# The experts' y in a convolutional decoder step: last two blocks kept on the chip, the rest added to x1 by accumulating DMAs

## What is computed

```python
x = x + concat(z_a, z_b) @ w_out                       # called x1 below
t = rmsnorm(x, g_ffn)                                  # called h2 below
grp  = argmax(coarse_logits)                           # 1 of 4 groups of 8 experts
top2 = top_k(fine_logits[grp], 2)
combine[token, expert] = softmax(top2) * p_grp         # two weights per token
out  = sum_e combine[:, e] * ((silu(t @ w_gate[e]) * (t @ w_up[e])) @ w_down[e])
y    = rmsnorm(x + out, g_final)
```

## Time and profile before

| | us |
|---|---|
| median of 3 runs | 563.7 (563.47 to 567.64) |
| the profiled execution's own time | 564.33 |
| its span in the profile | 562.6 |
| busy in the span: PE / DVE / POOL / ACT | 492.4 / 246.6 / 189.4 / 100.4 |
| mean granted TensorE clock, as a share of full speed | 0.966 |
| read from / written to DRAM | 134.47 MB / 13.17 MB |

### The profile page before, as it was taken

How to read it: one execution, slowest core, us unless ns; L and a number is a source line. 1 busy time by engine, 2 the same in 40 slices (tenths; PEclk the granted TensorE clock), 3 DMA queues, 4 the chain that set the end, 5 groups by cost and what they waited for, 6 DMA issues and landing times.

```text
span 562.6 us, 9132 instructions
## 1 busy us (share of the span) xinstructions
PE 492.4 (88%) x3423; PEld 294.4 (52%) x3424; DVE 246.6 (44%) x496; ACT 100.4 (18%) x204; POOL 189.4 (34%) x283
## 2 busy tenths in 40 slices
PE   6999999999999999996889889898877686498974
PEld 3887777777776455553344444444433343244431
DVE  4139999999955112347222212222121212022245
ACT  5131111011125332333111011110110101011113
POOL 2013818837678001112333333332323313033100
PEclk9999999999999999995899999999999989599998
DMA  8994016000002990149597999999999999998077
GB/s 331 307 395 88 0 24 276 2 0 1 1 1 97 401 379 37 40 130 394 181 348 266 369 379 408 383 401 385 395 373 384 400 389 399 400 404 332 29 260 252
DMA packets 35504, 141.17 MB, mean 251 GB/s; under 512 B 10322, under 2 KB 10338, under 8 KB 23193
## 3 DMA queue, kind: packets, MB, share of 16 engines
q1 hardware_dynamic: 29194, 127.91, 60.0%
q0 software_dynamic: 4960, 9.45, 5.2%
q10 hardware_dynamic: 1327, 3.49, 1.7%
HBM read 134.47 MB, written 13.17 MB: 262 GB/s over the span
## 4 chain that ended last, share of the span: by engine, by line
PE 67%; DMA 16%; issue 6%; SPq 4%; DVE 3%; ACT 2%; POOL 1%; DVEq 0%; POOLq 0%; ACTq 0%
PE bank L1226 25%; DMA region_w<-in_w_up 10%; PE bank L1309 9%; PE bank L1422 8%; PE bank L1442 7%; PE bank L1417 7%; DMA region_w<-in_w_in 3%; SPq L390 3%; DMA slot<-y_rows 2%; PE bank L1219 2%; PE bank L1408 2%; PE bank L1182 1%; PE bank L1432 1%; PE bank L1335 1%; PE bank L1370 1%
## 5 line engine op out<-in xcount | busy, mean ns | idle before, releaser
L1226 PE MATMUL bank<-region_h,region_w 128*128 128x256 f32 (+1 forms) x576 | 140.6, 406 | 0.0
L1226 PEld LDWEIGHTS bank<-region_h,region_w 128*128 128x128 f32 x576 | 109.2, 190 | 29.8
L1111 DVE TENSOR_TENSOR ua<-ua,bank 128x128 f32<-128x128 f32 x30 | 8.6, 287 | 184.0 <-ACT ua L621 184.0
L1422 PE MATMUL bank<-region_w,z 128*32 128x256 f32 x512 | 46.2, 419 | 16.6 <-DMA region_w<-in_w_up 14.2
L1309 PE MATMUL bank<-region_w,z 128*128 128x512 f32 x128 | 56.7, 596 | 0.2 <-ACT z L566 0.2
L1442 PE MATMUL bank<-region_w,ua 128*32 128x512 f32 x344 | 51.9, 598 | 0.0
L774 POOL COPY gcol<-gidx 64x1 uint32 (+1 forms) x30 | 5.4, 178 | 136.0 <-DVE sb_rows L1102 136.0
L909 DVE SCALAR_TENSOR_TENSOR z<-ub,par,z 128x512 f32<-128x512 f32 x60 | 47.5, 791 | 0.0
L909 DVE SCALAR_TENSOR_TENSOR region_x<-ub,par,region_x 128x512 f32<-128x512 f32 x56 | 46.5, 830 | 0.0
L705 POOL TENSOR_TENSOR ub<-region_x 128x512 f32<-128x512 f32 x4 | 25.3, 6332 | 58.7 <-ACT ub L520 32.0
L1309 PEld LDWEIGHTS bank<-region_w,z 128*128 128x128 f32 x128 | 23.8, 190 | 28.0 <-issue 26.3
(11 more groups left out here) (231 smaller groups left out, 657.3 us busy)
## 6 DMA issues: line engine op xcount, KB each, us to landing
region_w<-in_w_down SPq DMA_DIRECT2D x21, 1024.0 KB
region_w<-in_w_gate SPq DMA_DIRECT2D x16, 1024.0 KB
region_w<-in_w_up SPq DMA_DIRECT2D x16, 1024.0 KB
region_w<-in_w_in SPq DMA_DIRECT2D x4, 2048.0 KB, 19.1
slot<-in_w_gate SPq DMA_DIRECT2D x6, 1024.0 KB
slot<-in_w_up SPq DMA_DIRECT2D x6, 1024.0 KB
slot<-in_w_down SPq DMA_DIRECT2D x6, 1024.0 KB
region_x<-in_w_up SPq DMA_DIRECT2D x5, 1024.0 KB
```

The costliest lines, as they stand in the source:

```text
L1226: ins = mm(ps[2 * bank + j][:, 0:LEN[j]], sec[name][:, k, c * P:(c + 1) * P], hT[:, k, CUT[j]], start=(k == 0), stop=(k == KC - 1))
L1422: ins = mm(ps[1][r0:r0 + H, 0:2 * P].rearrange("p (w f) -> p w f", w=2), xT[:, k, half * H:(half + 1) * H], wgu[i][:, :, k, h, :], start=( ...
```

## The change

Each (token, choice)'s weight is applied when ACT copies y out of PSUM, not at the end. For that, `w12` is transposed on PE, copied by DVE to `wT`, stored by ACT to `w_dram` (four DMAs), and POOL gathers 128 weights of 4 bytes for each block (`weigh`, `weights`). `y_dram` is filled with zeros early (from a strip of slot 0 that POOL sets to zero, so expert 0's weights wait for it), x1 is also stored to `x1_dram`, and `yg`, `diag` and the work of PE, DVE and POOL on them are gone. The last two blocks are not scattered: their y stays in `yblk`. As soon as the other blocks' y has landed, POOL issues ten accumulating DMAs that add `y_dram` rows to x1 in SBUF (`add_rows`), and, for the 128 rows of the last two blocks, gathers of x1, y(k = 0) and y(k = 1) into `late`, the latter two accumulating (`fetch_late`). PE adds the on-chip y of the two blocks with 0/1 matrices `same[b]` (four matmuls), DVE adds that to `late`, and these rows are normed and scattered over the stored outputs, after all five tiles' stores have landed: tiles 0 to 4 hold these tokens without the last two blocks' y until then. DVE works out the tokens' numbers (`ilast`, 15 small operations) before its loop.

Cut to its core:

```diff
 # SP
+            sp.wait_ge(s_zero, 1)
+            sp.dma_start(y_dram.rearrange("(i p) d -> p i d", p=P),
+                         zero.unsqueeze(1).to_broadcast([P, 2 * NTOK // P, D])).then_inc(s_yz, 16)
+            sp.wait_ge(s_yz, 16)
             for part in range(2):
                 load_part(0, part, 0)
...
+            def store_x1(t):
+                sp.wait_ge(s_x1, 2 * t + 2)
+                sp.dma_start(x1_dram[t * P:t * P + TROWS[t], :], x1[0:TROWS[t], t, :]).then_inc(s_x1d, 16)
+            for t in range(NT - 1):
+                store_x1(t)
             sp.wait_ge(s_o, NT)
             load_expert(3, 3)
+            store_x1(NT - 1)
...
-            sp.wait_ge(s_ysc[1], pairs * 16)
-            sp.wait_ge(s_ysc[0], (pairs + odd) * 16)
-            for t, k in ((0, 0), (0, 1), (2, 0), (1, 0), (2, 1), (1, 1), (4, 0), (4, 1), (3, 0), (3, 1)):
-                sp.dma_start(yg[k][t][0:TROWS[t], :], y_dram[k * NTOK + t * P:k * NTOK + t * P + TROWS[t], :])\
-                  .then_inc(s_yg[k][t], 16)
 # ACT
+            act.wait_ge(s_wT, 1)
+            for k in range(2):
+                act.dma_start(w_dram[...], wT[...]).then_inc(s_wd, 16)     # twice for each k
...
+                act.wait_ge(s_wg[b], q * 16 + 16)
-                nc.scalar.activation(yblk[b], ps[3][:, :], ACT.Copy).then_inc(s_yc, 1)
+                nc.scalar.activation(yblk[b], ps[3][:, :], ACT.Copy, scale=wcol[:, b:b + 1]).then_inc(s_yc, 1)
...
+            for t in range(NT):
+                if t == BY_DVE:
+                    act.wait_ge(s_sqd, 1)
+                else:
+                    act.wait_ge(s_acc[t], 32)
+                    nc.scalar.activation(junk[0][0:n, :], x1[0:n, t, :], ACT.Square, accum_out=...)
+                root(t, n, s_rms3)
+            act.wait_ge(s_latex, 2)
+            nc.scalar.activation(junk[0], late, ACT.Square, accum_out=...)
+            root(NT, P, s_rms3)
 # POOL
+            pool.memset(wcol[:, :], 0.0).then_inc(s_const, 1)
+            pool.memset(zero, 0.0).then_inc(s_zero, 1)
...
+            def weigh(b, rows):
+                pool.indirect_dma_start(wcol[:, b:b + 1], None, w_dram[:, :],
+                                        bass.IndirectOffsetOnAxis(ap=rows, axis=0), ...).then_inc(s_wg[b], 16)
+            def weights(g, b, count):
+                pool.tensor_copy(vcol[:, b:b + 1], vidx[:, bass.ds(g, 1)]).then_inc(s_vc, 1)
+                pool.wait_ge(s_vc, count)
+                pool.tensor_tensor(carry[:, 3:4], carry[:, 1:2], carry[:, 1:2], ALU.add)
+                weigh(b, vcol[:, b:b + 1])
...
+            pool.wait_ge(s_wd, 64)
+            for b in range(2):
+                weigh(b, vidx[:, b:b + 1])
...
             with pool.Fori(0, pairs - 1) as h:
                 for b in range(2):
                     pool.wait_ge(s_mv, h * 2 + (b + 3))
                     gather(h * 2 + (b + 4), b)
                     scatter(h * 2 + b, b, h * 2 + (b + 2))
+                    weights(h * 2 + (b + 2), b, h * 2 + (b + 1))
-            for b in range(2):
-                scatter_last(b, b, pairs * 2 + b)
...
+            pool.wait_ge(s_ysc[1], lastp * 16)
+            pool.wait_ge(s_ysc[0], (lastp + odd) * 16)
+            def add_rows(t, k):
+                pool.dma_start(x1[0:n, t, :], y_dram[r:r + n, :], accum_op=ALU.add).then_inc(s_acc[t], 16)
+            fetch_late(x1_dram[:, :], 0, NTOK - 1)
+            for t in range(NT):
+                add_rows(t, 0)
+                if t == 2:
+                    pool.wait_ge(s_late, 16)
+                    fetch_late(y_dram[:, :], 0, 2 * NTOK - 1, compute_op=ALU.add)
+            for t in range(NT):
+                pool.wait_ge(s_acc[t], 16)
+                add_rows(t, 1)
+                if t == 0:
+                    pool.wait_ge(s_late, 32)
+                    fetch_late(y_dram[:, :], 1, 2 * NTOK - 1, compute_op=ALU.add)
+            pool.wait_ge(s_out, 16 * NT)
+            pool.wait_ge(s_nlate, 1)
+            for i, (dst, rows) in enumerate(((y_prompt[0], SEQ), (y_sample..., NS * SL))):
+                pool.indirect_dma_start(dst, ...ilast[:, 2 + i:3 + i]..., late, None, ...)
 # DVE
+            dve.wait_ge(s_wT_ps, 1)
+            nc.vector.tensor_copy(wT[:, :], ps[6][0:2 * NT, 0:P]).then_inc(s_wT, 1)
...
+            for t in range(NT):
+                normed(t, TROWS[t], x1[0:TROWS[t], t, :], s_norm[t])
+                if t == 1:
+                    dve.wait_ge(s_late, 48)
+                    for j in range(2):
+                        nc.vector.tensor_tensor(half, half, ps[4 + 3 * j][:, :], ALU.add).then_inc(s_latex, 1)
+            normed(NT, P, late, s_nlate)
 # PE
-            keep_busy(24)
+            keep_busy(6)
+            pe.wait_ge(s_w12, 1)
+            tr(ps[6][0:2 * NT, 0:P], w12, ident[:, :]).then_inc(s_wT_ps, 1)
+            keep_busy(17)
```

More of the change, by code:

```diff
@@ L115, in build_step @@
         hidT = ua_t[:, 2 * P:3 * P]
-        yg = [[(SLOT0 if k == 0 else RW)[:, t * D:(t + 1) * D] for t in range(NT)] for k in range(2)]
+        zero = SLOT0[:, 0:D]
+        late = RW[:, 0:D]
+        junk = [RW[:, D:2 * D], RW[:, 2 * D:3 * D]]
         ident = sb("ident", [P, P])
@@ L135, in build_step @@
         st_p = pst
-        diag = [[pst[:, (2 * i + k) * P:(2 * i + k + 1) * P] for k in range(2)] for i in range(len(BY_PE))]
+        dtok = pst[:, 0:P]
+        same = [pst[:, (1 + b) * P:(2 + b) * P] for b in range(2)]
+        wT = pst[0:2 * NT, 3 * P:4 * P]
         hist_t = sb("hist_b", [P, D])
@@ L468, in _ @@
                 sp.dma_start(dst, x1[0:TROWS[t], t, :]).then_inc(s_out, 16)
+            for i in range(2):
+                sp.wait_ge(s_olate[i], 16)
             sp.wait_ge(s_hout, 16 * 5)
@@ L662, in _ @@
+            act.wait_ge(s_latex, 2)
+            nc.scalar.activation(junk[0], late, ACT.Square, accum_out=small[:, 16 + NT:17 + NT]).then_inc(s_sq3, 1)
+            act.wait_ge(s_sq3, squared + 1)
+            root(NT, P, s_rms3)
         @block.gpsimd
@@ new lines, in _ @@
+            for t in range(NT):
[6 more added lines that the diff above has]
+            pool.wait_ge(s_nlate, 1)
+            for i, (dst, rows) in enumerate(((y_prompt[0], SEQ), (y_sample.rearrange("s l d -> (s l) d"), NS * SL))):
+                pool.indirect_dma_start(dst, bass.IndirectOffsetOnAxis(ap=ilast[:, 2 + i:3 + i], axis=0), late, None,
+                                        bounds_check=rows - 1, oob_is_err=False).then_inc(s_olate[i], 16)
@@ L1129, in _ @@
                 block_of(pairs, 0)
+            dve.wait_ge(s_trow, 1)
+            for b in range(2):
+                nc.vector.tensor_scalar(same[b], ps[6][:, 0:P], vlast[:, 3 + b:4 + b], None, ALU.is_equal).then_inc(s_same, 1)
             dve.wait_ge(s_gfin, 16)
-            def add_row(t, k):
-                n = TROWS[t]
-                dve.wait_ge(s_yg[k][t], 16)
-                if k:
-                    dve.wait_ge(s_fin1, t // 2 + 1)
-                nc.vector.scalar_tensor_tensor(out=x1[0:n, t, :], in0=yg[k][t][0:n, :],
-                                               scalar=w12[0:n, k * NT + t:k * NT + t + 1],
-                                               in1=x1[0:n, t, :], op0=ALU.mult, op1=ALU.add)\
-                    .then_inc(s_fin if k else s_fin1, 1)
@@ new lines, in normed @@
+            def normed(i, n, rows, done):
+                c = small[0:n, 40 + i:41 + i]
+                dve.wait_ge(s_rms3, i + 1)
+                nc.vector.reciprocal(c, c).then_inc(s_rstd3, 1)
+                dve.wait_ge(s_rstd3, i + 1)
+                nc.vector.scalar_tensor_tensor(out=rows, in0=rows, scalar=c, in1=gfin[0:n, :],
+                                               op0=ALU.mult, op1=ALU.mult).then_inc(done, 1)
+            for t in range(NT):
+                normed(t, TROWS[t], x1[0:TROWS[t], t, :], s_norm[t])
+                if t == 1:
+                    dve.wait_ge(s_late, 48)
+                    for j in range(2):
+                        dve.wait_ge(s_mix, j + 1)
+                        half = late[:, j * 512:(j + 1) * 512]
+                        nc.vector.tensor_tensor(half, half, ps[4 + 3 * j][:, :], ALU.add).then_inc(s_latex, 1)
```

170 lines of the change are left out of this document (86 added, 84 removed).

## The result

| | before | after |
|---|---|---|
| median, us | 563.59 (562.58 to 567.64, 4 runs) | 581.97 (580.59 to 584.37, 4 runs) |
| span of the profiled execution | 562.6 | 580.1 |
| mean granted clock | 0.966 | 0.935 |
| written to DRAM, MB | 13.17 | 20.78 |

The ratio is 1.0317 with an interval of [1.0256, 1.0378]: 18 us slower. The forecast was 564.5 with a range to 575, so it is wrong, and the time lies beyond its range. The direction of the miss is that of the rival "adds at twice the price" (573.0), and even that is 9 us short.

What follows compares the result with a forecast made beforehand. PE bounds it except 320 to 485 us, where the weights' stream does. Last add 551.4 plus 10.5 gives 561.9, plus 1.5 for the stream 563.4, +0.8 against 562.6; so median 563.7 + 0.8 = 564.5, range 555.5 to 575.

Steps and rivals of the forecast that it cites:

- adds at twice the price: Tail, slower rival: each accumulating tile costs 2.70 us, span up 9.3 us, median 573.0; chance 0.27 for twice or more.
- the stream's cost: Loop: the blocks' 4-byte weight gathers delay the full weights' stream by 1.5 us, within bounds of 1.4 and 8.1.
- an accumulating tile at 1.5 plain ones: Tail: an accumulating tile transfer takes 2.02 us against 1.35 plain, for 11 units; forecast case's chance 0.37.
- 0.5 of the end as now: End of the span: after the late rows' stores land, 0.5 us remains, as in the kernel before.
- my 4.7: Serial end: late's second issue 1.5 us, landing 2.35 plus 0.3, and 0.5 for the end, in all 4.7 us.
- adds at the price of plain transfers: Tail, faster rival: POOL's issuing is the floor, last add lands at 545.0, span down 5.6 us, median 558.1; chance 0.29.
- the upper bound of 8.1: Loop: most that the small weight packets could cost the stream, 8.1 us, at 53 ns of one engine each.
- the rival of dear weights: Loop, slower rival: small weight packets cost the stream 8.1 instead of 1.5 us, giving 571; chance 0.05.
- POOL's work per block, 5.9 us: Loop: POOL's work rises from 4.0 to 5.9 us per block of 8.7 us, so POOL still idles.
- The zero fill: Early stage: 4.7 MB of zeros takes 12.2 us, lands between 45 and 50 us, hidden before first use, cost 0.
- later than 284.3: Sign of being wrong: block 0's copy of y on ACT (L625) coming later than 284.3 us.
- Issue on POOL, 1.52 us each, as a floor: Tail: POOL issues 13 DMAs at a pitch of 1.52 us, so the last starts no earlier than 542.1.

Runs made afterwards that it cites:

- run 3: The kernel before with tile 3's store, its last, issued by POOL instead of SP; 566.44 us, ratio 1.008.
- run 4: The kernel before with one small add on POOL behind the last norm and no added DMA; 566.5 us, ratio 1.0062.
- run 6: The kernel before with one indirect gather of 64 rows on POOL behind the last norm; 569.75 us, ratio 1.0093.
- run 5: The changed kernel without the loop's 28 weight gathers, later blocks using the weights of blocks 0 and 1; 578.88 us, ratio 1.0271 to the kernel before.
- run 9: The changed kernel with only the first of its two late stores, to the prompt's rows; 578.5 us, ratio 1.0264 to the kernel before.
- run 12: The kernel before with 24 small direct DMAs by POOL behind its last scatter, nothing added at the end; 566.93 us, ratio 1.0077.
- run 2: The changed kernel without the late rows' two stores, SP waiting for late's norm instead; 570.75 us, ratio 1.0125 to the kernel before.
- run 1: The changed kernel with plain DMAs in place of the accumulating ones, each copy overwriting the one before; 569.27 us, ratio 1.0122 to the kernel before.
- run 11: The changed kernel without late rows, PE adding the last two blocks' y to each tile; seven accumulating DMAs, three plain loads; 560.71 us, ratio 0.9952 to before.
- run 7: The changed kernel without late rows, PE adding the last two blocks' y to each tile; all ten additions accumulating DMAs; 565.05 us, ratio 1.002 to before.
- run 8: The changed kernel without late rows, PE adding the last two blocks' y to each tile; eight accumulating DMAs, two plain loads; 561.75 us, ratio 0.997 to before.

## Why the prediction was wrong

Its sum for the tail against the profile:

| step | predicted | measured | difference |
|---|---|---|---|
| POOL's first issue of the tail | 523.9 | 525.28 | +1.4 |
| from there to the last add in SBUF | 27.5 | 36.7 | +9.2 |
| to the last tile's store landed (567.96) | 5.8 | 5.9 | +0.1 |
| to the start of POOL's second late issue | 1.5 | 2.3 | +0.8 |
| to the end of the span | 3.2 | 9.9 | +6.7 |

That is 18.2 us; 1.5 of it the forecast had as the stream's cost, so the span missed by 16.7 (563.4 against 580.1). Two steps make up 11.8 of it: the price of an add (5.1) and the end of the span (6.7).

**The step that failed first: an accumulating tile at 1.5 plain ones.** It was called the least certain number, bounded by 1.35 and 2.70 us, and set at 2.02 on the picture of three passes where a plain transfer has two. Measured: 0.524 MB / 211 GB/s = 2.48 us, 1.84 times a plain one, against the upper bound. Eleven tiles make that 5.1 us of the 9.2. The other 4.1 are smaller terms. At the start the share is 0.65 from 524 to 534, that is 3.5 us of idle time, 2.2 of them behind the first issue, where the forecast had 1.1 and then data without a gap. SP's stores moved 1.32 MB by 562.0, 3.4 us at 388 GB/s, for 2. The slow stretch from 546 to 550 (153 GB/s) costs 1.1, and 0.5 is left. The Trainium skill's Collectives: The Full Stack, in its section on the bandwidth ceiling, gives two source reads as the reason why a reduce-scatter runs at half the rate of an all-gather, and a measured ratio of 1.93; the 1.84 here is near it. No run here tells a second read from the add itself. The rival "adds at twice the price" had a chance of 0.27. It had the price nearly right, and was still 9 us short, as it had the same end as the forecast.

**The step that failed second: "0.5 of the end as now".** It was read from a profile in which POOL's drain ended with SP's last landing and so cost nothing. I never asked what lies under the end of the span, and so moved POOL's last instruction from well before the end to the very end without its price. The landing of late's stores was right (570.22 to 572.7, 2.5 us for 2.65). Behind it come 7.2 us of drain: 5.2 us that follow POOL's last instruction with 62 or 63 DMAs, whatever it is (runs 3, 4 and 6), and 3.5 for the 43 DMAs that the change gives POOL (runs 5, 9 and 12), less the 1.5 of the landing that runs beside them (571.24 to 572.7). Run 2 prices the whole serial end at 11.2 us for my 4.7. The rival "adds at the price of plain transfers" had the same fault: run 1 is that case, and it took 569.3, not 558.1. Its last landing, 545.0, was right (546.0 in run 1); from there to the last store landed it was 7.5 us for 5.8, with DVE as the bound, and behind that 12.1 (553.5 to 565.6) for 4.7.

**Weights in the loop, 1.5 us.** Of run 5's 3.1 us by the medians, 28 x 0.08 = 2.3 are the drain, so some 0.8 is left for the stream and the rest of the loop; the upper bound of 8.1 and the rival of dear weights are out. The rule on packets under 512 B (the Trainium skill's DMA: Bandwidth & Descriptors, Specifications) had put the cost near that bound; the stream's 386 GB/s with the gathers and 387 without don't bear that out. ACT never waited for a weight. POOL's work per block, 5.9 us, came out as computed and cost nothing.

**Stages ahead.** The zero fill was hidden: it landed at 53.5 (28.14 + 25.4), not 45 to 50, w_fine followed at 54.95, and the first use is at 94.4. SP's w_out was issued at 83.0 for 81.8. Block 0's copy came at 285.46, and "later than 284.3" was to be a sign of being wrong; these 1.2 us are those of the first wait for w_in, so the table's stage itself added nothing that shows.

**Issue on POOL, 1.52 us each, as a floor.** That was the pitch of indirect gathers. Direct DMAs took 0.53 to 0.57 us plain (run 1) and 0.83 to 0.94 accumulating (run 7; up to 1.2 in the changed kernel), so the floor was lower; what held POOL back was its wait for landings (6.70 us at 542.78).

## What to carry to other kernels

An accumulating DMA into SBUF saves an engine's addition but here cost 1.84 plain transfers. In these runs it paid only as far as the DMA engines were idle anyway; on the path, mix it with plain loads and an engine's additions until neither waits (run 11). Before POOL is given the last act of a kernel, or more DMAs anywhere in it, look at the rows of the program's last line: its closing drain starts behind its last instruction, grew with the number of DMAs that it had issued and with adds still under way, and is free only while another engine ends later. A part that is done again by itself, serially, behind everything else, is priced from the end of the span and not from its own instructions.

## What the runs showed of the hardware that I had not expected

- With the engines full (share 1.06 to 1.07), accumulating DMAs from DRAM to SBUF in float32 with rows of 4 KB move 211 GB/s, where plain ones between the same places on the same queue reach 389 to 393.
- POOL's closing drain ends 5.2 us behind its last instruction where it issued 62 DMAs in the program, and 0.08 us later for each further one (8.7 us at 105), for 4-byte gathers (run 5) as for direct DMAs of a 4 KB row (run 12). In run 12 the further ones had been issued by 544.0, 10 us before POOL's last operation. With accumulating DMAs still under way it ends later, 9.3 to 17.4 us behind the last instruction (runs 2, 7, 8 and 11).
- Issuing a direct DMA of 128 rows on POOL took 0.53 to 0.57 us (run 1), an accumulating one 0.83 to 0.94 us (run 7), and an accumulating indirect one 1.66 us (changed kernel) where the plain one took 1.08 (run 1).
